# Sparse attention in head pairs: logits of two heads from the two halves of the rows, values computed transposed

## The reference, cut to what matters

```python
def block(args):
    ...
    _, sel = lax.top_k(score, n_sel)
    ...
    logits = jnp.einsum('bqgrd,bqkgd->bqgrk', qg, k_sel).astype(jnp.float32) * (d ** -0.5)
    logits = logits - slopes[None, None, :, :, None] * dist[:, :, None, None, :]
    logits = jnp.where((dist >= 0)[:, :, None, None, :], logits, -jnp.inf)
    p = jax.nn.softmax(logits, axis=-1).astype(v.dtype)
    o = jnp.einsum('bqgrk,bqkgd->bqgrd', p, v_sel)
...
mix = jnp.concatenate([ret, att], axis=-1) * mix_scale
x = x + g1[:, None, :] * (mix @ w_o)
```

## Time and profile before

| | before |
|---|---|
| median of 3 runs | 1673.68 us (1672.87 to 1678.42) |
| the profiled execution | 1675.41 us, of which the span from first to last instruction 1673.6 |
| busy: TensorE, VectorE, ScalarE, GpSimd | 94%, 82%, 67%, 21% of the span |
| chain that ended last: TensorE, VectorE, ScalarE, transfers | 84%, 9%, 3%, 2% |
| mean granted clock of TensorE | 0.937 of full speed |

### The profile page before, as it was taken

The page is one execution under the profiler, slowest core; times in us unless marked ns, Lnnn a source line. Parts: engine busy times, 40 slices in busy tenths (PEclk is TensorE's granted clock), DMA queues, the critical chain, the costliest instruction groups (busy, mean ns, idle before and its releaser), DMA issues.

```text
span 1673.6 us, 20929 instructions
## 1 busy us (share of the span) xinstructions
PE 1574.7 (94%) x7032; PEld 1241.6 (74%) x7032; DVE 1379.7 (82%) x1162; ACT 1125.2 (67%) x1173; POOL 343.2 (21%) x261
## 2 busy tenths in 40 slices
PE   3999989999689999999999999999999999999975
PEld 2678966656468888888888888888888888888862
DVE  4689944316679999999999999999999999999965
ACT  3544344324368888888888878788888888887841
POOL 1214410010102222222222322222222222232210
PEclk8999985599689999999999999999999999999998
DMA  9745310023469989999998999998899999899927
GB/s 349 218 151 192 136 64 0 1 70 138 143 250 365 366 341 357 357 366 367 363 368 339 367 365 372 363 367 346 347 362 371 361 369 366 334 363 366 365 102 260
DMA packets 97856, 478.98 MB, mean 286 GB/s; under 512 B 24408, under 2 KB 33728, under 8 KB 45504
## 3 DMA queue, kind: packets, MB, share of 16 engines
q1 hardware_dynamic: 86848, 456.76, 70.5%
q0 software_dynamic: 10976, 21.81, 3.6%
HBM read 475.37 MB, written 20.98 MB: 297 GB/s over the span
## 4 chain that ended last, share of the span: by engine, by line
PE 84%; DVE 9%; ACT 3%; DMA 2%; issue 1%; SPq 0%; DVEq 0%; POOLq 0%; POOL 0%; ACTq 0%
PE bank L1323 14%; PE bank L1324 14%; PE bank L1322 14%; PE bank L1344 7%; PE bank L1346 7%; PE bank L1345 7%; PE bank L1206 3%; PE bank L1151 2%; PE bank L1172 2%; PE bank L1304 2%; PE bank L1315 2%; PE bank L1296 2%; DVE w_lo L1445 2%; DMA ring<-in_ada_w 1%; PE bank L1159 1%; PE bank L1037 1%
## 5 line engine op out<-in xcount | busy, mean ns | idle before, releaser
L1484 DVE TENSOR_TENSOR e_lo<-ring,e_hi 128x2048 fp32r<-128x2048 f32 x384 | 868.5, 2289 | 79.9 <-ACT e_hi L717 75.5
L717 ACT ACTIVATE e_hi<-ring 128x2048 fp32r<-128x2048 f32 x384 | 729.9, 1918 | 192.3 <-PE bank L1324 189.2
L1322 PE MATMUL bank<-e_hi,x_hi 128*128 128x512 f32 x1024 | 407.5, 398 | 1.5 <-DVE e_lo L1484 1.5
L1323 PE MATMUL bank<-e_lo,x_hi 128*128 128x512 f32 x1024 | 404.1, 395 | 0.0
L1324 PE MATMUL bank<-e_hi,x_lo 128*128 128x512 f32 x1024 | 403.1, 394 | 0.0
L1322 PEld LDWEIGHTS bank<-e_hi,x_hi 128*128 128x128 f32 x1024 | 193.6, 189 | 48.6 <-DVE e_lo L1484 2.4
L1323 PEld LDWEIGHTS bank<-e_lo,x_hi 128*128 128x128 f32 x1024 | 193.4, 189 | 42.2
L1324 PEld LDWEIGHTS bank<-e_hi,x_lo 128*128 128x128 f32 x1024 | 193.2, 189 | 41.5
L1344 PE MATMUL bank<-e_hi,act_hi 128*128 128x512 f32 x512 | 208.8, 408 | 4.9 <-DVE act_lo L1497 4.9
L1345 PE MATMUL bank<-e_lo,act_hi 128*128 128x512 f32 x512 | 202.8, 396 | 0.0
L1346 PE MATMUL bank<-e_hi,act_lo 128*128 128x512 f32 x512 | 202.7, 396 | 0.0
(11 more groups left out here) (245 smaller groups left out, 1930.9 us busy)
## 6 DMA issues: line engine op xcount, KB each, us to landing
ring<-in_w_gu SPq DMA_DIRECT2D x256, 1024.0 KB, 6.8
ring<-in_w_down SPq DMA_DIRECT2D x128, 1024.0 KB, 7.5
ring<-in_ada_w SPq DMA_DIRECT2D x24, 1024.0 KB, 7.7
ring<-in_w_in SPq DMA_DIRECT2D x9, 1024.0 KB, 6.4
ring<-expert_rows SPq DMA_DIRECT2D x6, 1024.0 KB, 10.8
ring<-in_w_o SPq DMA_DIRECT2D x4, 1024.0 KB, 6.3
ring<-in_w_in SPq DMA_DIRECT2D x10, 256.0 KB, 5.9
xs<-in_x SPq DMA_DIRECT2D x4, 512.0 KB, 5.2
```

What stands on the lines that cost most here:

```text
L717: return nc.scalar.activation(dst, src, ACT.Copy, scale=scale)
L1322: pe.matmul(bank[b][:], x_hi[:, c, :], hi, start=False, stop=False)
L1323: pe.matmul(bank[b][:], x_hi[:, c, :], lo, start=False, stop=False)
L1484: tt(e_lo[c % PARTS][:], raw(period.raw_slot(c)), e_hi[:, c % PARTS, :].bitcast(F32), ALU.subtract).then_inc(lo_ready, 1)
```

## The change

Heads are taken in the pairs `PAIRS` (0,5), (1,4), (2,7), (3,6), one head from each group, and the four pairs in turn go over the four blocks of rows: 16 steps i = 4q + t. Head b of a pair lies in rows 64b to 64b + 63 of the array, so the two logits of a step use different halves. What else differs:

- The queries are scaled by 1/SLOPE[h] besides the 1/8 (`q_scale`, eight small memsets on GpSimd), so that one VectorE instruction (`tensor_tensor_reduce` in `biased`) adds `neg`, multiplies by -SLOPE and takes the minimum, where two stood.
- VectorE divides the probabilities by their sums before they are transposed (`normalised`), so nothing is left to divide afterwards.
- Of the two transposed heads of a step ScalarE copies one out and VectorE the other (both functions are called `turned`), into `prT`, which holds whole heads.
- The values of a pair are computed once for all four blocks (`values(q)`), with the values as weights (64 columns) and up to 512 columns of probabilities streamed. The result comes out transposed, in the half of the partitions that `hT` wants, and is copied there by `values_out`. The transposes of the attention's result are gone; those of the retention's (`turn_retention`) stand at i = 16, ahead of the last three `turn_probs`.
- The logits use banks 0 to 3 and so TensorE waits for the retention's last copy (`ro_taken`) before the first logits; before, only the first values waited for it.
- Four buffers of a pair's probabilities instead of three of a head's; the retention's products begin at step 5 of 16 instead of 12 of 32, and the square root at step 3 instead of 8.

```diff
+PAIRS = [(q, 4 + (q ^ 1)) for q in range(4)]
+STEPS = 4 * T
+TURN_LAG, VALUE_LAG = 3, 5
-RET_FROM = 12
+RET_FROM = 5
...
+        prT = nc.alloc_sbuf_tensor_at("prT", [P, 4, T, S], F32, offset=-(-nc.sbuf_base // 32) * 32)
...
-                take(QUERY[m], aqT[:, m, :], HD ** -0.5)
+                take(QUERY[m], aqT[:, m, :], q_scale[:, m:m + 1])
...
+            def probs(i):
+                w = (i % T + 1) * P
+                for b in range(2):
+                    a.wait_ge(logits_taken, 2 * i + b + 1)
+                    p = pr[:, i % 4, b, 0:w]
+                    nc.scalar.activation(p, p, ACT.Exp, scale=-1.0, bias=nmax[:, i % 4, b:b + 1],
+                                         accum_out=psum_[:, i % 4, b:b + 1]).then_inc(prob_ready, 1)
+            def values_out(half):
+                a.wait_ge(values_full, 2 * half + 2)
+                for n in range(2):
+                    k = 4 + 2 * n + half
+                    copy(hT[:, k, :], bank[6 + n][:], vecT[:, 64 + k:65 + k]).then_inc(values_taken, 1)
...
+            def logits(i):
+                q, t = divmod(i, T)
+                for b in range(2):
+                    u = 2 * i + b
+                    if u >= 4:
+                        pe.wait_ge(logits_taken, u - 3)
+                    lo = HD * b
+                    pe.matmul(bank[u % 4][:, 0:(t + 1) * P], aqT[lo:lo + HD, q, t * P:(t + 1) * P],
+                              akT[lo:lo + HD, 0:(t + 1) * P], start=True, stop=True).then_inc(logits_full, 1)
+            def turn_probs(i):
+                t = i % T
+                for b, taken in enumerate((turned_even, turned_odd)):
+                    pe.wait_ge(norm_ready, 2 * i + b + 1)
+                    if i > 0:
+                        pe.wait_ge(taken, i)
+                    for m in range(t + 1):
+                        mm = pe.transpose(bank[4 + b][:, m * P:(m + 1) * P], pr[:, i % 4, b, m * P:(m + 1) * P],
+                                          ident[:])
+                    mm.then_inc(turned_full, 1)
+            def values(q):
+                pe.wait_ge(turned_even, T * q + T)
+                pe.wait_ge(turned_odd, T * q + T)
+                if q == 2:
+                    pe.wait_ge(values_taken, 2)
+                for m in range(T):
+                    for b, h in enumerate(PAIRS[q]):
+                        at = HD * (h % 2)
+                        mm = pe.matmul(bank[6 + b][at:at + HD, m * P:S], av[:, m, b * HD:(b + 1) * HD],
+                                       prT[:, 2 * (q % 2) + b, m, m * P:S], start=(m == 0), stop=(m == T - 1))
+                mm.then_inc(values_full, 1)
...
+            pe.wait_ge(ro_taken, RH)
+            for i in range(STEPS + VALUE_LAG):
+                if i < STEPS:
+                    logits(i)
+                if i == STEPS:
+                    pe.wait_ge(logits_taken, 2 * STEPS)
+                    pe.wait_ge(ret_ready, T * RH)
+                    for k in range(RH):
+                        turn_retention(k)
+                if TURN_LAG <= i < STEPS + TURN_LAG:
+                    turn_probs(i - TURN_LAG)
+                if i >= VALUE_LAG and (i - VALUE_LAG) % T == T - 1:
+                    values((i - VALUE_LAG) // T)
...
+            def biased(i):
+                q, t = divmod(i, T)
+                w = (t + 1) * P
+                if i >= 4:
+                    v.wait_ge(turned_full, 2 * i - 6)
+                for b, h in enumerate(PAIRS[q]):
+                    u = 2 * i + b
+                    v.wait_ge(logits_full, u + 1)
+                    nc.vector.tensor_tensor_reduce(out=pr[:, i % 4, b, 0:w], in0=bank[u % 4][:, 0:w],
+                                                   in1=neg[:, NEG_AT[t]:NEG_AT[t] + w], scale=-SLOPE[h], scalar=3.0e38,
+                                                   op0=ALU.add, op1=ALU.min,
+                                                   accum_out=nmax[:, i % 4, b:b + 1]).then_inc(logits_taken, 1)
+            def normalised(i):
+                w = (i % T + 1) * P
+                v.wait_ge(prob_ready, 2 * i + 2)
+                nc.vector.reciprocal(pinv[:, i % 4, :], psum_[:, i % 4, :]).then_inc(inv_ready, 1)
+                v.wait_ge(inv_ready, i + 1)
+                for b in range(2):
+                    p = pr[:, i % 4, b, 0:w]
+                    ts(p, p, pinv[:, i % 4, b:b + 1], None, ALU.mult).then_inc(norm_ready, 1)
```

More of the change, by code:

```diff
@@ L71 @@
 A_RV = A_RK + 2
[L72 to L74 removed]
+A_MIX = A_RV + 2 * T
+A_H2 = A_MIX + RH
 D_RG = 0
@@ L1142, in _ @@
                 mm.then_inc(ro_full, 1)
-            order = [(t, h) for t in range(T) for h in range(AH)]
-            def logits(n):
-                t, h = order[n]
-                lo = HD * (h // 4)
-                dfree(D_QK + n)
-                pe.matmul(dbank(D_QK + n)[:, 0:(t + 1) * P], aqT[lo:lo + HD, h % 4, t * P:(t + 1) * P],
-                          akT[lo:lo + HD, 0:(t + 1) * P], start=True, stop=True).then_inc(dve_full, 1)
-            def turn_probs(n):
-                t, h = order[n]
-                free(A_PT + n)
-                pe.wait_ge(prob_ready, n + 1)
-                for m in range(t + 1):
-                    mm = pe.transpose(abank(A_PT + n)[:, m * P:(m + 1) * P], pr[:, n % 3, m * P:(m + 1) * P],
-                                      ident[:])
-                mm.then_inc(act_full, 1)
@@ L1163, in values @@
-            def values(n):
-                t, h = order[n]
-                if h == 0 and t >= 2:
-                    pe.wait_ge(pv_taken, t - 1)
-                if n == 0:
-                    pe.wait_ge(ro_taken, RH)
-                pe.wait_ge(act_taken, A_PT + n + 1)
-                g = h // 4
-                for m in range(t + 1):
-                    mm = pe.matmul(bank[3 + 4 * (t % 2)][:, h * HD:(h + 1) * HD], prT[:, n % 3, m * P:(m + 1) * P],
-                                   av[:, m, g * HD:(g + 1) * HD], start=(m == 0), stop=(m == t))
-                mm.then_inc(pv_full, 1)
@@ L1175, in _ @@
-            for n in range(len(order) + 4):
-                if n < len(order):
-                    logits(n)
-                if 2 <= n < len(order) + 2:
-                    turn_probs(n - 2)
-                if n >= 4:
-                    values(n - 4)
-            for k in range(KD):
+            def logits(i):
[7 more added lines that the diff above has]
+                              akT[lo:lo + HD, 0:(t + 1) * P], start=True, stop=True).then_inc(logits_full, 1)
@@ L1543, in _ @@
                        decay[:, h, 0:RS_W[m]], ALU.mult).then_inc(dve_taken, 1)
-            order = [(t, h) for t in range(T) for h in range(AH)]
-            def rows(t):
-                v.wait_ge(prob_ready, AH * (t + 1))
-                done(nc.vector.reciprocal(pinv[:, :, t:t + 1], psum_[:, :, t:t + 1]))
-                v.wait_ge(pv_full, AH * (t + 1))
-                tt(att[:, t, :].rearrange("p (h d) -> p h d", h=AH),
-                   bank[3 + 4 * (t % 2)][:].rearrange("p (h d) -> p h d", h=AH),
-                   pinv[:, :, t:t + 1].broadcast_to((P, AH, HD)), ALU.mult).then_inc(pv_taken, 1)
@@ L1567, in _ @@
+            v.wait_ge(ro_full, RH)
+            for i in range(STEPS + TURN_LAG):
+                if i < STEPS:
+                    biased(i)
+                if i == RET_FROM:
                     v.wait_ge(ro_summed, 1)
                     done(nc.vector.reciprocal(ri[:], rt[:]))
-                for r in range(2 * (n - RET_FROM), 2 * (n - RET_FROM) + 2):
+                for r in range(2 * (i - RET_FROM), 2 * (i - RET_FROM) + 2):
                     if 0 <= r < T * RH:
@@ L1573, in _ @@
                             op0=ALU.mult, op1=ALU.mult).then_inc(ret_ready, 1)
-                if h == 4 and t >= 1:
-                    rows(t - 1)
-            rows(T - 1)
+                if 1 <= i < STEPS + 1:
+                    normalised(i - 1)
+                if i >= TURN_LAG:
+                    turned(i - TURN_LAG)
             v.wait_ge(g1_in, 16)
```

119 lines of the change are left out of this document (59 added, 60 removed).

## The result

| | before | after |
|---|---|---|
| median of 4 runs (lowest to highest) | 1674.77 us (1672.87 to 1678.42) | 1623.24 us (1622.43 to 1626.79) |
| profiled execution, its span | 1675.41, 1673.6 | 1622.43, 1620.7 |
| mean granted clock of TensorE | 0.937 | 0.960 |

The ratio is 0.9687, 95% interval 0.9669 to 0.9706: 51 us less, where 22 were forecast (1651.5, range 1634 to 1668).

What follows compares the result with a forecast made beforehand. TensorE at half clock was taken to bound the old attention. Taking the longer of VectorE and TensorE per iteration gave 79.3 us, the output projection 22.1 us earlier: 1653.3 profiled, 1651.5 median, range 1634 to 1668.

Steps and rivals of the forecast that it cites:

- What bounds the kernel now: Old attention and mix, about 101 us: bound by what TensorE issues at 1.2 GHz, with VectorE waiting for it.
- The clock: TensorE in the new attention: half clock at first, rising inside each values(q) for one more iteration, full from i = 16.
- Rival 1: Attention at full clock nearly throughout, so VectorE binds: 66.3 us up to the output projection, 1638.5 us in all; chance 0.20.
- VectorE's terms: VectorE's work per attention iteration, 2.4 to 3.6 us, 48 us in all; it binds wherever the clock is 1.0.
- A lone pair of logits: Two heads' logits in opposite row halves overlap partly, three records instead of four: 1.08, 1.73, 2.37, 3.00 us by width.
- The values: A pair's eight value calls in alternating column halves overlap: 6.0 us at half clock, 2.9 at full; otherwise 10.9 and 4.9.
- Rival 3: Attention values do not overlap, clock as in the sum: +2.3 us for each of three, +2 for the last, 1660; chance 0.14.
- Rival 4: VectorE's new add-and-minimum instruction takes two cycles an element: about half of 10.7 us shows, 1657 us; chance 0.06.
- The tables: VectorE's wait for exponentials behind the square root's two ScalarE table loads: 1.5 us at half clock, 2.6 at full.
- The end: After the 16 iterations: remaining transposes, values(2), values(3) and last copies before the output projection, 14.8 us.
- Rivals 2 and 5: Attention at half clock throughout: 2, values overlapping, 1667 us, chance 0.12; 5, values one behind the other, 1686, chance 0.08.
- I count a microsecond saved before the output projection as one saved in all: Behind 343.94 us everything hangs on the mix and nothing waits for a fixed time, so savings before it carry through fully.

## Why the prediction was wrong

The direction was right and the size was less than half of what came. By its steps:

1. **What bounds the kernel now**: right. The old stage was TensorE at 1.2 GHz nearly throughout, and its length fell by 45.6 us when only the height of the logits was changed, so that the clock came back.
2. **The clock: the step that failed.** "The new kernel begins like the old one, with short logits and waits, so I expect half clock there too", with a rise only inside each `values(q)` that lasts for one iteration. Measured: 0.68 over the first 15 us, so the beginning was right, and 0.95 behind them. The clock came back at about 256.5 us, behind the pairs of logits of 256 and 384 columns, ahead of `values(0)` (262.08), and stayed; only in `values(1)`, 3.95 us at 273.67, did it fall to half. So it didn't need the values' long rows. The sum gave the paired logits no part in the clock; I took the low clock for the work of short calls and waits. It went with calls that occupy 64 of the 128 rows: without a pause they left the clock at 0.50, and full-height calls in the same order, or half-height ones in opposite halves next to each other, had it at 1.0 for most of the stage. Rival 1 was the right case; its reason ("the retention held 1.0 with pauses") was not the one that the runs show, and its 66.3 us were too long as well. The price by its sum is 13 us of the 24.
3. **VectorE's terms: mis-sized.** The durations were right but for the reciprocal's, and the sum of 48 us was not: busy time is 37.3, since an instruction starts 0.08 us ahead of the end of the one before it, and the accumulator's read is free. The idle terms (tables, values, hand-overs) were near what came. This is the other 11 us, by difference: no run separates it. That VectorE paces the new stage was right in the main (14.6 us for the second pass).
4. **A lone pair of logits**: 1.5 calls were assumed. It takes 1.16 and 1.63 us at half clock, one call. The Trainium skill's page "TensorEngine Tiling (Array Packing)", section Theoretical Speedup, gives up to 2x where a small dimension is at most 64. This trace agrees: 1.16 us for the pair of 256 columns, 1.15 for one call. The 6.5 us that this was priced at belong to a low clock, which the kernel kept only in its beginning; where the logits could not overlap at all and the clock was up, the stage was 0.6 longer.
5. **The values**: overlap was right, 2.30 us where 2.9 was forecast at full clock, and 3.90 by heads. Rival 3 falls; apart they cost 7.3, in part by the clock, where it had 8.9 more.
6. **The new instruction on VectorE**: 684 ns at 512 columns against 0.69, no slower than the plain addition (688). Rival 4 falls. **The tables**: 1.5 to 2.6 forecast, 1.9 measured. **The end**: 11.9 for 14.8, at a clock of 1.0; rival 1 had 12.1.
7. **Rivals 2 and 5** fall with the clock. One term of the sum, 3.1 for i = 4, should be 3.0 by its own rule; it changes nothing.
8. **"I count a microsecond saved before the output projection as one saved in all"**: the loop behind did not stay as it was. Its 6.7 us came from addresses, as the run with these alone shows (6.9). No step thought of that.

**Where the rest of the change's work is gone.** The paired order alone makes the old stage 57.6 us, and the whole new structure makes it 57.8. It takes less from TensorE (41.4 busy of 55.2) and adds to VectorE, whose work is then on the path; in the old structure at full clock VectorE is busy for 15.6 of 16 us at first (260 to 276), and then TensorE is without a pause (276 to 296). Two ways that end at the same length. Without anything side by side the stage is 24 us shorter than before (79.7 against 103.9), with the clock back from the first values on; these are not there on top of the pairs' gain, as the 57.6 shows.

**What stays open**: whether in the kernel before with paired logits the head order alone would do, without the two calls together; how the 15.3 us of the pair set apart divide; the 11 us of VectorE, which rest on a difference; what sets the two levels of the kernel with extra work; and which tensor's address, by which rule, makes an expert 36.09 or 36.36 us.

## What to carry to other kernels

Before planning around a busy TensorE, look at its granted clock beside its busy time: 99% busy at 0.50 is a kernel that waits for its clock, and calls that use half the array's rows should first be put side by side in opposite halves, here another order of heads and one call moved ahead. Add up VectorE's work by the distance from start to start in the timeline, not by durations. And when tensors ahead of a long loop change in size, compare one iteration of the loop: a few tenths of a microsecond in each can be the placement. The kernel before with its tensors at the new addresses shows it.

## What was not expected of the hardware

- TensorE at 99% busy for 90 us (89.35 of 90.00) with a clock of 0.50, while the same sequence with 128 rows instead of 64 ran at 1.00 (247.7 to 294 us, 42.7 of 46.3 us busy). The Trainium skill's page "TensorE: Matmul & The Clock Gate", Part 1, says that the clock is set by how busy TensorE has been recently. These two runs disagree, if busy means time without a gap: the busier one had the lower clock.
- Half- and full-height calls in turn that end at either of two times: 1651 us in two runs, 1680 and 1683 in two, of one and the same kernel, at mean clocks of 0.964 and 0.946.
- Tensors moved by 32 bytes: an expert of 36.09 us became 36.36, the kernel some 9 us slower; by 160 bytes the other way from before, 36.30 became 36.09.
- VectorE's accumulator read (82 ns) and 0.08 us of each instruction's end cost nothing when work follows.
